# Gate and up weights of an expert pair in two 2 MB transfers instead of four 1 MB transfers

## The reference

```python
def hierarchical_moe(h, w_rg, b_rg, w_re, b_re, w_gate, w_up, w_down):
    # top-1 of 4 groups, then top-2 of its 8 experts: 2 of 32 experts for each token
    ...
    for grp in range(N_GROUPS):
        sl = slice(grp * EXPERTS_PER_GROUP, (grp + 1) * EXPERTS_PER_GROUP)
        hid = silu(einsum('td,edf->tef', hf, w_gate[sl])) * einsum('td,edf->tef', hf, w_up[sl])
        y = y + einsum('tef,efd->td', hid * combine[:, sl, None], w_down[sl])
```

## Time and profile before

| | |
|---|---|
| median of three runs | 1678.85 us |
| the profiled execution, its own time | 1680.54 us |
| its span, first to last instruction | 1678.6 us |
| mean granted TensorE clock | 0.970 |
| expert stage, first gate_up to last down | 1301.06 to 1592.42 us |
| TensorE busy over the span | 1560.0 us (93%) |

### The profile page before, as it was taken

How to read it: one execution, slowest core, us unless ns; L and a number is a source line. 1 busy time by engine, 2 the same in 40 slices (tenths; PEclk the granted TensorE clock), 3 DMA queues, 4 the chain that set the end, 5 groups by cost and what they waited for, 6 DMA issues and landing times.

```text
span 1678.6 us, 20983 instructions
## 1 busy us (share of the span) xinstructions
PE 1560.0 (93%) x7452; PEld 1133.3 (68%) x7452; DVE 809.5 (48%) x1472; ACT 617.5 (37%) x1182; POOL 137.9 (8%) x156
## 2 busy tenths in 40 slices
PE   5989999989999999999999998999997999999947
PEld 4777778745787888888887887777785333333336
DVE  4766764577334666664324354654456122222263
ACT  4556543367324455553223313454335200000122
POOL 0004200010000000000000001000001122221100
PEclk9999999999999999999999999999998999999969
DMA  5232233221232333333323322221243999999331
GB/s 183 69 128 90 73 120 95 60 73 39 72 98 76 96 99 94 100 94 97 99 82 102 100 70 63 70 69 59 86 170 137 407 411 400 388 386 369 129 150 50
DMA packets 93168, 232.93 MB, mean 139 GB/s; under 512 B 15952, under 2 KB 16208, under 8 KB 88864
## 3 DMA queue, kind: packets, MB, share of 16 engines
q1 hardware_dynamic: 79296, 209.75, 36.3%
q0 software_dynamic: 13072, 21.77, 3.9%
q10 hardware_dynamic: 720, 0.33, 0.1%
HBM read 282.05 MB, written 16.84 MB: 178 GB/s over the span
## 4 chain that ended last, share of the span: by engine, by line
PE 84%; DVE 9%; ACT 3%; issue 1%; DMA 1%; POOL 1%; SPq 0%; ACTq 0%; DVEq 0%; POOLq 0%
PE ps L341 20%; PE ps L343 19%; PE ps L342 19%; PE ps L958 10%; PE ps L977 5%; PE ps L940 1%; DVE lo L336 1%; PE ps L444 1%; DVE acc L1929 1%; PE ps L1594 1%; PE ps L1582 1%; PE ps L1568 1%; PE ps L544 1%; PE ps L1446 1%; DVE HTl L409 1%
## 5 line engine op out<-in xcount | busy, mean ns | idle before, releaser
L336 DVE TENSOR_TENSOR lo<-raw,hi 128x512 fp32r<-128x512 f32 x304 | 208.6, 710 | 313.8 <-ACT hi L330 313.2
L330 ACT ACTIVATE hi<-raw 128x512 fp32r<-128x512 f32 x304 | 184.8, 632 | 383.8 <-PE ps L343 382.4
L341 PE MATMUL ps<-HTh,lo 128*128 128x512 f32 x688 | 274.3, 399 | 20.0 <-DVE HTl L409 6.4
L342 PE MATMUL ps<-HTl,hi 128*128 128x512 f32 x688 | 271.6, 395 | 0.0
L343 PE MATMUL ps<-HTh,hi 128*128 128x512 f32 x688 | 271.5, 395 | 0.0
L341 PEld LDWEIGHTS ps<-HTh,lo 128*128 128x128 f32 x688 | 131.4, 191 | 50.9 <-DVE HTl L409 12.4
L343 PEld LDWEIGHTS ps<-HTh,hi 128*128 128x128 f32 x688 | 131.6, 191 | 28.1
L342 PEld LDWEIGHTS ps<-HTl,hi 128*128 128x128 f32 x688 | 131.6, 191 | 27.1
L341 PE MATMUL ps<-hi,HTl 128*128 128x512 f32 (+1 forms) x352 | 139.0, 395 | 2.3 <-ACT sq L617 2.0
L343 PE MATMUL ps<-hi,HTh 128*128 128x512 f32 (+1 forms) x352 | 135.2, 384 | 0.0
L342 PE MATMUL ps<-lo,HTh 128*128 128x512 f32 (+1 forms) x352 | 135.1, 384 | 0.0
(11 more groups left out here) (378 smaller groups left out, 2514.5 us busy)
## 6 DMA issues: line engine op xcount, KB each, us to landing
raw<-in_wstream SPq DMA_DIRECT2D x384, 256.0 KB, 2.7
slot<-in_wexp SPq DMA_DIRECT2D x64, 1024.0 KB, 14.0
slot<-in_wexp SPq DMA_DIRECT2D x16, 2048.0 KB, 15.0
cum<-cum_d POOLq DMA_DIRECT2D x16, 256.0 KB, 3.4
fcb<-fc_d POOLq DMA_DIRECT2D x16, 256.0 KB, 3.7
YG<-ye_d SPq DMA_DIRECT2D x4, 1024.0 KB, 8.8
X<-in_x SPq DMA_DIRECT2D x4, 512.0 KB, 5.6
xg_d<-xn POOLq DMA_DIRECT2D x4, 512.0 KB, 4.3
```

The source lines that it names most:

```text
L330: act.activation(hi[:, i % RING, :], raw[:, i % RING, :], ACT.Copy).then_inc(hi_ready, 1)
L336: dve.tensor_tensor(lo[:, i % RING, :], raw[:, i % RING, :], hi[:, i % RING, :].bitcast(F32), ALU.subtract).then_inc(lo_ready, 1)
L341: pe.matmul(o, al, bh, start=start, stop=False)
L342: pe.matmul(o, ah, bl, start=False, stop=False)
```

## The change

Gate and up weights of a main tile come in two transfers of 2 MB, each with contiguous runs of 8 KB, where there were four of 1 MB with runs of 4 KB. The waits are made coarser with them: SP issues each half after TensorE has used the same half of the tile two earlier, and TensorE waits once for each half. The count that `unit_used` reaches for a tile falls from 4 to 2. The first pair's transfers wait for two units less of the streamed weights (`MOE_AT - 6` in place of `MOE_AT - 4`). Down weights, overflow weights and the order of all DMAs stay.

```diff
-PIECES = 4
+PIECES = 2
+CHUNKS = DC // PIECES
...
-                    if j < MAIN and c % 2 == 0:
-                        pe.wait_ge(raw_full[(j * PIECES + c // 2) % RING], 16 * ((MOE_AT + j * PIECES + c // 2) // RING + 1))
+                    if j < MAIN and c % CHUNKS == 0:
+                        u = j * PIECES + c // CHUNKS
+                        pe.wait_ge(raw_full[u % RING], 16 * ((MOE_AT + u) // RING + 1))
...
-                    if j < MAIN and c % 2 == 1:
+                    if j < MAIN and c % CHUNKS == CHUNKS - 1:
                         mm.then_inc(unit_used, 1)
...
-                    sp.wait_ge(lo_ready, MOE_AT - PIECES)
+                    sp.wait_ge(lo_ready, MOE_AT - RING + PIECES)
...
-                    sp.dma_start(slots[j % 2][:, :, 2 * i:2 * i + 2, :].rearrange("p e c n -> p e (c n)"),
-                                 both[j][:, :, 1024 * i:1024 * i + 1024]).then_inc(raw_full[(j * PIECES + i) % RING], 16)
+                    sp.dma_start(slots[j % 2][:, :, CHUNKS * i:CHUNKS * i + CHUNKS, :].rearrange("p e c n -> p e (c n)"),
+                                 both[j][:, :, 512 * CHUNKS * i:512 * CHUNKS * (i + 1)]).then_inc(raw_full[(j * PIECES + i) % RING], 16)
```

## The result

The change makes the kernel slower by 0.35%: 1685.52 us (1682.31 to 1689.38, 8 runs) against 1679.70 us (1677.85 to 1681.09, 8 runs), ratio 1.0035, 95% interval 1.0026 to 1.0044. The forecast was 1707 us, with a range from 1688 to 1722 us: the direction is right, the size is not.

A forecast was written before the change was run, and what follows sets the result against it. TensorE was taken to set the pace. Gather waits of 20.3 us plus 9 us of low clock made 29 us, taken as 28, on a median 1.7 us below the profiled 1680.54: 1707 us, range 1688 to 1722.

The forecast's parts named there:

- nothing to gain: Expert stage: TensorE is busy throughout a 12.00 us tile and never waits for a weight, so faster weights shorten nothing.
- Rival C: Expert weight stream: DMA engines are the real limit and larger packets relieve them; 4.1 us faster, 1675 us; chance 0.04.
- The coarser waits: Main tiles' gate and up weights: 4.4 us later together, against about 10 us to spare; costs nothing.
- what is late next: Overflow tiles: weight gathers land later, so TensorE waits at L958 before six tiles, 2.8 to 4.1 us each.
- the turns: DMA queues q0 and q1 alternate record for record; q0 falls from 99.5 to 51 records a us beside 8 KB packets.
- the queue is full: q1 has work throughout the overflow gathers' 430 records, so the second gather lands 4.1 us later; waits sum to 20.3 us.
- The term of tile 1: Wait before overflow tile 1: 4.1 us shift plus 0.1 us to first matmul, less 0.8 us spare.
- The clock: Low clock behind the new waits: 1.0 us for each of four, 2.5 us for each of two, 9 us in all.
- the clock needs an idle time of a certain length: Low stretches behind TensorE's waits: reason to favour the lower ends and take 28 us in place of 29.
- Rival B: Overflow gathers: GpSimd's issue rate and 4 us to first record hold most of their 7 us; nothing moves, 1679 us; chance 0.07.
- rival A: Overflow gathers late, but clock stays up or shift is nearer 3 us; 9 to 20 us more, 1688 to 1699; chance 0.18.

## Why the prediction was right, and where it was wrong

**Right: nothing to gain.** Chain, waits and landings said that TensorE sets the pace of the stage. The two kernels without gathers are equal, and no tile fell under 12 us. Rival C had no place to act. The coarser waits were costed at nothing and cost nothing.

**Right: what is late next.** The waits stand at the line and for the DMA that were named, before four of the six tiles that were named. Undoing the cause in three ways (4 KB packets with coarse waits, another order on GpSimd, no gathers) gave the time of before each time.

**Right: the turns.** One record of q0 for one of q1, 53.6 a us beside 8 KB packets against 51 forecast. The Trainium skill (DMA: Bandwidth & Descriptors, section Queues, rings and completion order) has the round robin, and the runs agree. Its 9 to 17 descriptors for a turn they do not show: 375 records stood against 376.

**Wrong: that the queue is full.** The step that failed is "So the queue is full over the gathers' records even if nothing older is left in it." It added up megabytes and compared them with a stretch of time, and left out when they arrive: the half is issued 1.8 us later than the first quarter was, and no DMA moves anything at the moment of its issue (the smallest ones take 2.1 us to land with q1 empty). In the changed kernel the queue is full before overflow tile 1. Before tiles 2 to 6, in both profiled executions, some engines have no q1 packet for a moment, just when the records come, and 205 to 250 of the 430 pass in a microsecond. The sum of waits was 7.0 us in place of 20.3, and with one more transfer on q1, and no burst, it was 18.6. The term of tile 1, 3.4 us, was 2.35 us: 53.6 records a us pass, not 51, and the second landing moved by 3.1 us, not 4.1. That the coarser release makes the gap is shown with 4 KB packets only. With 8 KB packets it is argued from that, and from the gap's place 0.8 to 1.4 us behind the issue of the half. If so, the coarser release is a help against the packets that it comes with.

**The clock followed from that.** 9 us were forecast for six waits near 3 and 4 us. Four waits of 0.9 to 2.35 us came, with one low stretch: 1.7 us. Where six waits of 2.2 to 3.9 us did come, the clock cost 8.6 us. The forecast's remark that the clock needs an idle time of a certain length is not borne out: a wait of 2.19 us was followed by a low stretch, and waits of 2.37, 2.60 and 2.74 us were not. And the forecast had no term for the part behind the stage. The 2.4 us that it saved were luck for the kernel. Without them the median would have been some 1688 us (an estimate, 1685.5 + 2.4), at the range's lower end.

**Rival B** named the right quantity, how fast the records pass. Of its two reasons, the 4 us to the first record is seen again in the second gather (4.2 to 4.6 us), and the issue rate of GpSimd no run tests. It foresaw no moment at which q1 has too little to send. The range's lower end lay 2.5 us too high, since rival A took its waits from a shorter shift in all six tiles, and none of the cases had a shift in some of the tiles only.

Not settled: why the second gather, once its records start, takes 3.3 us in one tile and 5.4 in another, so that tile 2 waited 2.04 us in spite of its burst and tiles 3 and 5 did not wait. No run here takes that apart.

No kernel that was tried beats the one before. The changed kernel with the gathers ahead of the scatter equals it.

## What to carry to other kernels

Before making the packets of a bulk stream larger, look for small or indirect DMAs that run beside it and have little time to spare: what they need is turns, and a turn is as long as the other queue's packet. Count their records (rows that are skipped count too), and read the rate from a window in which both queues have work. And when a cost hangs on a queue being busy, check it in time, from issue to first packet, not by its bytes: here the same kernel with a transfer more on q1 lost 27.3 us where it lost 5.8 without. If such a DMA is late, its place among its own queue's DMAs is the cheapest thing to change.

## What the runs showed of the hardware that was not expected

- A skipped row of an indirect DMA still takes a turn: 430 records that carry 0.00 MB are what the 8 KB packets slowed down. In the changed kernel, with q1 busy, the first record of the second gather stands 4.2 to 4.6 us behind its issue. With q1 empty the whole gather lands in 2.1 us.
- Two streams of matmuls with 64 output rows each, alternating between the two halves of the array's columns, took 7.09 us for 32; four of one half and then four of the other took 8.97 us.
- The clock behind TensorE's idle times: 2.04 us left it at 1.00 once and 2.74 us once (the changed kernel), 2.37 and 2.60 us left it too (with the added transfers), while 2.19 and 2.35 us were followed by 3.4 us at 1.2 GHz. The low stretch behind an idle time of 2.8 us late in the kernel is there before the change and missing after it, with the same instructions around it, and it is worth 2.4 us.
